# Second layer: the first up-projection tile behind each mixer's norm, multiplied before the norm is known

## The reference, cut to what matters

```python
x = layer_norm(DN_ALPHA * x + m, mix_ln_g[i], mix_ln_b[i])
x = layer_norm(DN_ALPHA * x + swiglu(x, ffn_w_in[i], ffn_w_down[i]), ffn_ln_g[i], ffn_ln_b[i])

def layer_norm(x, g, b):
    mu = jnp.mean(xf, -1, keepdims=True)
    var = jnp.mean(jnp.square(xf - mu), -1, keepdims=True)
    return ((xf - mu) * lax.rsqrt(var + LN_EPS) * g + b).astype(x.dtype)

def swiglu(x, w_in, w_down):
    gate, up = jnp.split(x @ w_in, 2, axis=-1)
    return (jax.nn.silu(gate) * up) @ w_down
```

## Time and profile before

| what | value |
|---|---|
| median of 3 runs | 2448.66 us (2447.87 to 2449.31) |
| the profiled execution: own time | 2454.04 us |
| the profiled execution: span | 2452.3 us |
| PE busy | 2388.9 us, 97% of the span |
| DVE busy | 1755.6 us, 72% |
| ACT busy | 1180.0 us, 48% |
| mean clock | 0.99 |

### The profile page before, as it was taken

How to read it: one execution, slowest core, us unless ns; L and a number is a source line. 1 busy time by engine, 2 the same in 40 slices (tenths; PEclk the granted TensorE clock), 3 DMA queues, 4 the chain that set the end, 5 groups by cost and what they waited for, 6 DMA issues and landing times.

```text
span 2452.3 us, 49456 instructions
## 1 busy us (share of the span) xinstructions
PE 2388.9 (97%) x19026; PEld 2208.2 (90%) x19026; DVE 1755.6 (72%) x2902; ACT 1180.0 (48%) x1828; POOL 75.6 (3%) x149
## 2 busy tenths in 40 slices
PE   8999999999999999989999999999989999989998
PEld 6877877778998999988999998999889999988998
DVE  4788799988857875776666767665567657776665
ACT  4454522223655444566444555444555446466444
POOL 1000001000000000000400000000000000000000
PEclk9999999999999999999999999999999999999999
DMA  8433355555434555332555532555424554322653
GB/s 311 160 110 122 107 193 180 191 180 164 171 105 144 192 180 164 132 102 70 184 181 183 175 110 79 185 181 188 157 87 164 188 174 158 116 87 84 199 177 132
DMA packets 119715, 378.31 MB, mean 154 GB/s; under 512 B 11655, under 2 KB 29063, under 8 KB 119184
## 3 DMA queue, kind: packets, MB, share of 16 engines
q1 hardware_dynamic: 107040, 328.62, 40.6%
q0 software_dynamic: 12528, 47.62, 5.8%
HBM read 375.15 MB, written 1.05 MB: 153 GB/s over the span
## 4 chain that ended last, share of the span: by engine, by line
PE 77%; DVE 12%; issue 6%; ACT 3%; DMA 1%; DVEq 1%; SPq 0%; ACTq 0%
PE gb L610 20%; PE gb L611 19%; PE gb L612 19%; DVE w_lo L579 2%; PE mb L719 1%; DVE W L1629 1%; PE mb L610 1%; PE mb L612 1%; PE mb L611 1%; DVE W L2743 1%; DMA X<-in_x 1%; ACT w_hi L571 1%; DVE W L1253 1%; DVE W L1254 1%; PE gb L691 1%
## 5 line engine op out<-in xcount | busy, mean ns | idle before, releaser
L610 PE MATMUL gb<-Xs,w_hi 128*128 128x256 f32 (+1 forms) x3422 | 1037.4, 303 | 10.1 <-DVE w_lo L579 4.2
L612 PE MATMUL gb<-Xs,w_lo 128*128 128x256 f32 (+1 forms) x3422 | 1023.7, 299 | 0.0
L611 PE MATMUL gb<-Xs,w_hi 128*128 128x256 f32 (+1 forms) x3336 | 994.8, 298 | 0.0
L571 ACT ACTIVATE w_hi<-raw 128x1024 fp32r<-128x1024 f32 x582 | 610.7, 1057 | 694.4 <-PE gb L612 652.4
L579 DVE TENSOR_TENSOR w_lo<-raw,w_hi 128x1024 fp32r<-128x1024 f32 x582 | 706.1, 1223 | 211.2 <-ACT w_hi L571 201.0
L610 PEld LDWEIGHTS gb<-Xs,w_hi 128*128 128x128 f32 x3422 | 646.4, 189 | 57.7 <-issue 17.5
L612 PEld LDWEIGHTS gb<-Xs,w_lo 128*128 128x128 f32 x3422 | 646.4, 189 | 26.1
L611 PEld LDWEIGHTS gb<-Xs,w_hi 128*128 128x128 f32 x3336 | 630.3, 189 | 23.4 <-issue 1.9
L611 PE MATMUL gb<-Fs,w_hi 128*128 128x256 f32 (+1 forms) x966 | 278.3, 288 | 0.0
L610 PE MATMUL gb<-Fs,w_hi 128*128 128x256 f32 (+1 forms) x880 | 248.4, 282 | 0.7 <-ACT Pj L1778 0.7
L612 PE MATMUL gb<-Fs,w_lo 128*128 128x256 f32 (+1 forms) x880 | 247.3, 281 | 0.0
(11 more groups left out here) (472 smaller groups left out, 3233.7 us busy)
## 6 DMA issues: line engine op xcount, KB each, us to landing
raw<-in_up SPq DMA_DIRECT2D x264, 512.0 KB, 3.5
raw<-in_down SPq DMA_DIRECT2D x96, 512.0 KB, 3.7
R<-in_mod_later POOLq DMA_DIRECT2D x80, 512.0 KB, 3.8
raw<-in_gdn_in SPq DMA_DIRECT2D x64, 512.0 KB, 3.5
raw<-in_down SPq DMA_DIRECT2D x48, 384.0 KB, 4.2
raw<-in_hgrn_in SPq DMA_DIRECT2D x32, 512.0 KB, 4.4
raw<-in_ev_in SPq DMA_DIRECT2D x24, 512.0 KB, 4.4
raw<-in_gla_in SPq DMA_DIRECT2D x24, 512.0 KB, 3.5
```

Source lines behind the costliest of these rows:

```text
L571: nc.scalar.activation(hi, raw[:, slot, 0:hi.shape[1]] if len(hi.shape) == 3 else like(raw[:, slot], hi), ACT.Identity).then_inc(*hi_ready ...
L610: nc.tensor.matmul(to, weight_block(w_slot, 0, k), x_hi, start=start, stop=False)
L611: nc.tensor.matmul(to, weight_block(w_slot, 0, k), x_lo, start=False, stop=False)
L612: return nc.tensor.matmul(to, weight_block(w_slot, 1, k), x_hi, start=False, stop=stop)
```

## The change

For each of the four mixers:

- ACT writes g times `X[m]` into a part of `Fs` behind each square (`act_gained`), DVE the low part of the same (`dve_gained`), for all 8 rows, one row behind in `dve_out`. Two columns with g and b are appended, so that a row has 258 columns.
- PE multiplies tile 0 with these rows directly behind the sums (`pe_gained`). The warming products behind the mixers are gone. The group behind the norm is tiles 1, 2, 3.
- Behind the last row DVE splits one weight tile more (tile 3), before `dve_ln`.
- `act_ln` ends with a copy of the mean from PSUM (`mean_kept`).
- In the feed-forward part the first pair is taken out of the loops of ACT and DVE. DVE corrects tile 0 with mean and root (`dve_late_norm`), and ACT's first silu reads the corrected tile, with W^T b as its bias.

```diff
-        def pe_features(pe, tiles, n, ready=None, by_seq=False):
+        def pe_features(pe, tiles, n, ready=None, by_seq=False, gain=False):
...
-            if ready:
+            if gain:
+                pe_gained(pe)
+                pe_group(pe, 1, n, ready)
+            elif ready:
                 pe_group(pe, 0, n, ready)
...
-            for u in range(AHEAD if ready or by_seq else 0, peel):
+            for u in range(SLOTS if gain else AHEAD if ready or by_seq else 0, peel):
                 tile(u)
...
                 nc.scalar.activation(squares_at(m, T) if m else sq_sum(T), X[:, m, 0:T], ACT.Square, scale=1 / 32).then_inc(*sq_ready.inc())
+                if mixer is not None:
+                    act_gained(act, "mix", mixer, m)
...
+        GN = T + 2
+        gained = lambda part, m, n=GN: Fs[:, KC * part + m, 0:n]
+
+        def gain_columns(which, i, part):
+            at = VC[f"{which}_g"]
+            both = vec[:, at:at + VC[f"{which}_b"] - at + 32].rearrange("p (a c) -> p c a", a=2)
+            return Fs[:, KC * part:KC * part + KC, T:GN], both[:, KC * i:KC * i + KC, :]
+
+        def act_gained(act, which, i, m):
+            if m == 0:
+                to, of = gain_columns(which, i, 0)
+                nc.scalar.activation(to, of, ACT.Identity)
+            nc.scalar.activation(gained(0, m, T), X[:, m, 0:T], ACT.Identity, scale=ln_gain(which, i, m)[0]).then_inc(*gain_hi.inc())
+
+        def dve_gained(dve, which, i, m):
+            dve.wait_ge(*gain_hi.due("dve"))
+            if m == 0:
+                to, of = gain_columns(which, i, 1)
+                nc.vector.tensor_tensor(to, of, gain_columns(which, i, 0)[0], ALU.subtract)
+            nc.vector.scalar_tensor_tensor(out=gained(1, m, T), in0=X[:, m, 0:T], scalar=ln_gain(which, i, m)[0], in1=gained(0, m, T),
+                                           op0=ALU.mult, op1=ALU.subtract).then_inc(*gain_rows.inc())
+
+        def pe_gained(pe):
+            pe.wait_ge(*lo_ready.due("pe"))
+            pe.wait_ge(*gemm_taken.free("pe"))
+            for k in range(KC):
+                pe.wait_ge(*gain_rows.due("pe"))
+                last = pe_block(gb[:, 0, 0:GN], 0, k, gained(0, k), gained(1, k), k == 0, k == KC - 1)
+            last.then_inc(*gemm_out.inc())
+
+        def dve_late_norm(dve):
+            acc, mean, to = gb[:, 0, :], W[:, 2, T:2 * T], W[:, 6, 0:T]
+            dve.wait_ge(*gemm_out.due("dve"))
+            nc.vector.tensor_scalar(small[:, 158:159], acc[:, T:T + 1], -1.0, None, ALU.mult).then_inc(*dve_step.inc())
+            nc.vector.tensor_copy(small[:, 159:160], acc[:, T + 1:T + 2])
+            dve.wait_ge(*dve_step.sent())
+            dve.wait_ge(*mean_kept.due("dve"))
+            link(dve, nc.vector.scalar_tensor_tensor(out=to, in0=mean, scalar=small[:, 158:159], in1=acc[:, 0:T], op0=ALU.mult, op1=ALU.add))
+            nc.vector.tensor_tensor(to, to, W[:, 3, T:2 * T], ALU.mult).then_inc(*late_normed.inc())
...
+            if which == "mix":
+                nc.scalar.activation(W[:, 2, T:2 * T], mb[:, 2, 0:T], ACT.Identity, scale=1.0 / D).then_inc(*mean_kept.inc())
...
                 dve_sums(dve, m, T, layer is None)
+                if mixer is not None and m:
+                    dve_gained(dve, "mix", mixer, m - 1)
                 if 3 <= m < KC - 1:
                     dve_tile(dve)
+            if mixer is not None:
+                dve_gained(dve, "mix", mixer, KC - 1)
+                dve_tile(dve)
...
-                    dve_tile(dve)
-                    here = gemm_out.due("dve")
+                    if late:
+                        dve_late_norm(dve)
+                    else:
+                        dve_tile(dve)
+                        here = gemm_out.due("dve")
...
+                    if first and u == 0:
+                        act.wait_ge(*late_normed.due("act"))
+                        nc.scalar.activation(W[:, 4, 0:n], W[:, 6, 0:n], ACT.Silu, bias=small[:, 159:160]).then_inc(*silu_done.inc())
+                    else:
+                        nc.scalar.activation(W[:, 4 + u, 0:n], src, ACT.Silu).then_inc(*silu_done.inc())
...
-            pe_out(pe, T, lambda k: None if k % 2 else pe.wait_ge(*gn_applied.due("pe")), layer_norm=True, aside=OUT_ASIDE)
+            pe_out(pe, T, lambda k: None if k % 2 else pe.wait_ge(*gn_applied.due("pe")), layer_norm=True, warm=0, aside=OUT_ASIDE)
```

46 lines of the change are left out of this document (27 added, 19 removed).

## The result

| | before | after |
|---|---|---|
| median of 5 runs | 2448.02 us (2444.01 to 2449.31) | 2458.73 us (2449.64 to 2464.63) |
| profiled execution: own time, span, mean clock | 2454.04, 2452.3, 0.990 | 2449.64, 2447.9, 0.991 |
| group of output tiles to tile 4, four mixers | 40.57, 40.57, 40.42, 40.41 us | 42.07, 41.96, 41.43, 41.98 us |

The account below looks back on a forecast made before the run. PE, 97% busy, was taken as the bound, with tile 4's start after each mixer as the cost. Chain +1.6 us and clock +2.3 us made +3.9, from 2448.66 to 2452.6 us, range 2446 to 2458.5.

Parts of the forecast that it names:

- at nothing I cost: Output tiles before the norm: the 8 high and 8 low parts fit beside them, DVE under 2.8 us a tile; no cost.
- step 1: DVE before the last residual: row 5's low part now precedes the split there, so the residual is 0.15 us late.
- 5, high part of tile 4 behind the last sum: ACT after the norm: mean copy and table load use up 1.05 us of slack; high part starts 0.4 us late.
- 6, wait before tile 4: PE after tile 3: tile 4 starts 0.4 us later, so PE waits 3.1 us where it waited 0.55.
- clock: PE's new waits bring half clock behind two of four mixers, 1.15 us each: +2.3 us.
- have become longer: Sign that the forecast is wrong: the output tiles before the norm are longer; 0.1 us each if DVE did not keep up.
- Step 3: DVE before the norm: row 7's low part and the split of tile 3 precede the variance, making it 1.15 us late.
- Half clock after the 1.9 us wait costs nothing: PE's group behind the norm: even at half clock it would end at 1171.8, before tile 4 can start at 1173.4.
- The idea works: Rival, chance 0.07: tile 4 isn't bound by ACT and DVE, starts 2.3 us earlier a mixer; 9.2 us gained, 2439.5.
- the chain might be shorter: Rival, chance 0.13: split doesn't delay the variance, or tile 4's high part starts by 1168.5; down to -3 us, 2445.7.
- The correction was never late: Rival, chance 0.05, claimed DVE's correction of tile 0 puts the silu 1 us later; +5.6 us without the clock, 2454.3.
- The clock holds: Rival, chance 0.25: PE waits of 3.1 us between dense stretches leave the clock at 1.00; +1.6 us, 2450.3.

Follow-up runs that it names:

- the seventh experiment: Changed kernel with ACT's and DVE's programs reordered, no work left out; three series: 2446.95, 2441.55 and 2444.80 us, ratios 0.999, 0.9969, 0.9978 of before.
- the first experiment: Changed kernel with 2 warming products put back behind tile 0 and 3 behind tile 3; 2455.86 us against 2449.89, ratio 1.002.

## Why the prediction was right or wrong

The direction and the middle of the chain were right; the size was not, by 4.7 of 8.6 us, 3.9 of it in the chain (5.5 against 1.6). By the ratio the changed kernel stands 8.6 us over before, 2457.2 from the median that the prediction started at, inside its range; by its own median it is 0.2 us outside. That the range reaches so far is luck: it was made wide for the clock, and what filled it was mostly a delay that the prediction had put at nothing. The step that failed is the one "at nothing I cost", with step 1 as its end.

| step | forecast, us | measured, us | |
|---|---|---|---|
| 1, and the low parts "at nothing": last residual | +0.15 | +1.46, +1.28, +0.89, +1.44 | failed |
| 2, high part of a row | 0.5 | 0.49 | right |
| 3, variance behind the last sum | +1.15 | +1.24, of which the split 1.13 | right |
| 4, wait before the group | 1.9 | 1.81 | right |
| 5, high part of tile 4 behind the last sum | +0.4 | +0.47 (13.66 against 13.19) | right |
| 6, wait before tile 4 | 3.1 | 2.53; 1.2 where the group is slow | 0.6 too long |
| tile 4, four mixers | +1.6 | +5.5 | failed by step 1 |
| clock | +2.3 | 0.7 to 3.7 | open |

Counted from the last sum tile 4 is 0.2 to 0.3 us later, not even the 0.4; the rest is that the last sum itself is late (24.77, 24.73, 24.19, 24.75 against 23.50, 23.66, 23.50, 23.50).

**The failed step.** The working was "0.42 x 3 + 1.22, and 0.42 is added: 2.9 less overlaps of 0.09 each, under 2.8". Measured it is 2.85, over the 2.81 of most of PE's tiles. Five overlaps of 0.09 would even make 2.45: the overlap isn't there between the residual and the two sums, where the next operation starts 0.46 and 0.52 us behind one of 0.42 (1149.72, 1150.18 and 1150.70 in the trace of before). And the question was wrong too. A row of DVE that had been waiting 0.3 us each tile was taken as free time; it was the rate at which DVE worked off what it owes when three tiles end at once. The aside "the first three rows come at once but the next tile's bank is long free" looked at PE's side only. What the prediction named as its sign, output tiles that "have become longer", was looked for in the wrong quantity as well: PE's tiles kept their 2.8 us, and only the last residual shows the arrears. The experiment without low parts shows the cause, as the residual went back to 22.83; that it takes both the low parts and the late start is seen there too, since ACT's 0.51 alone is made up for.

**Step 3.** The delay is right, and the split is its size, but the reason is a chain of two: the low part waits 0.49 for ACT and keeps the split behind it. Put the other way round, as in the seventh experiment, the split fills the wait and the variance is only 0.43 to 0.48 late.

**The clock.** "Half clock after the 1.9 us wait costs nothing" was right, seen at two norms in one profile and at all four in another. Half clock behind the second wait came once in four, not twice, and at 1.5 us, in a profile whose clock was the best of its five runs. The prediction did not see that the first takes from the second: a group at half clock eats half of the wait before tile 4, and at the six places where it did no half clock followed there. What the clock cost in the time stays open (0.7 to 3.7 us).

**The rivals.** "The idea works" fails as forecast, since ACT's order forbids it; the rival that the chain might be shorter (down to -0.75 a mixer) is what the kernel without low parts has, -0.8 to -1.1. The correction was never late: L1127 ends 1.0 us before the silu. "The clock holds" is the first experiment, which by a chain of 1.6 should have been 2451.5 beside its own before and was 2455.9; this tells apart chain and clock most plainly. The 0.8 us by which it let the group start earlier came from reading the group's second matmul as its first; this cost the sum nothing, as the chain decides. Of the chances, "slower" is given 0.39, where the three parts named for it add to 0.35.

**The table load.** It takes 1.28 us and the next operation starts 0.02 behind it, so the trace goes against the drain of about 1.4 us that the Trainium skill ("ScalarE: Activation LUTs", "What ACT_TABLE_LOAD costs") adds. Its rule of idle gaps ("TensorE: Matmul & The Clock Gate", "HAM oscillation — how this bites in real kernels") would not have had half clock behind 1.81, 2.45 or 2.54 us either; the traces show it.

## What to carry to other kernels

A short wait of an engine in every round is not spare time if the engine starts its rounds in arrears: sum the whole stage from its first row, with the work added, and look when the last row comes out. Work moved forward into filler gains only as much as the other engines' chain to the next work gets shorter, so shorten that chain first; here the orders of two engines, with no work left out, turned +8.6 us into -2.4 to -7.6. And where an operation has to wait anyway (the low part for ACT), put the long one that is ready before it, not behind.
